# Plain-head attention scores as split products, with the rotary parts stacked on both halves of the partitions

## What is computed

```python
def mla_attention(q_nope, q_pe, k_nope, k_pe, v):
    scale = (q_nope.shape[-1] + q_pe.shape[-1]) ** -0.5

    def block(args):
        qn, qr = args
        s = (jnp.einsum('bqhd,bkhd->bhqk', qn, k_nope)
             + jnp.einsum('bqhr,bkr->bhqk', qr, k_pe)).astype(jnp.float32) * scale
        p = jax.nn.softmax(s, axis=-1).astype(v.dtype)
        return jnp.einsum('bhqk,bkhd->bqhd', p, v)
```

## Time and profile before

| | us |
|---|---|
| median of 3 runs | 2017.85 |
| lowest and highest | 2015.47, 2018.05 |
| profiled execution, its own time | 2011.72 |
| its span in the profile | 2009.9 |
| mean granted clock | 0.995 |
| busy: PE, DVE, ACT, POOL | 1893.5, 762.4, 612.0, 628.7 |

### The profile page before, as it was taken

How to read it: one execution, slowest core, us unless ns; L and a number is a source line. 1 busy time by engine, 2 the same in 40 slices (tenths; PEclk the granted TensorE clock), 3 DMA queues, 4 the chain that set the end, 5 groups by cost and what they waited for, 6 DMA issues and landing times.

```text
span 2009.9 us, 22143 instructions
## 1 busy us (share of the span) xinstructions
PE 1893.5 (94%) x8716; PEld 1220.1 (61%) x8716; DVE 762.4 (38%) x1551; ACT 612.0 (30%) x1111; POOL 628.7 (31%) x374
## 2 busy tenths in 40 slices
PE   5999999999989989989999999899899999999998
PEld 3554337634333333368887868544577678888786
DVE  6552266523222222262899225366340220000002
ACT  3112562311011011062223344466343342232212
POOL 0000432011011010054443325555434235555532
PEclk9999999999999999999999999999999999999999
DMA  9452003889999999963224321110142023322321
GB/s 383 168 211 87 32 22 131 316 359 426 428 427 427 428 428 428 396 217 111 84 84 126 105 84 67 49 33 22 64 157 84 1 95 101 109 84 88 122 84 63
DMA packets 90037, 358.29 MB, mean 178 GB/s; under 512 B 6955, under 2 KB 35883, under 8 KB 75484
## 3 DMA queue, kind: packets, MB, share of 16 engines
q1 hardware_dynamic: 87088, 351.75, 45.1%
q0 software_dynamic: 2304, 4.20, 0.6%
q10 hardware_dynamic: 556, 1.13, 0.1%
HBM read 355.42 MB, written 5.83 MB: 180 GB/s over the span
## 4 chain that ended last, share of the span: by engine, by line
PE 75%; DMA 13%; DVE 5%; ACT 3%; issue 2%; POOL 1%; SPq 0%; POOLq 0%; DVEq 0%; ACTq 0%
PE bank L754 14%; PE bank L756 14%; PE bank L755 14%; PE bank L729 11%; DMA slots<-in_w_expert_gate 9%; PE bank L1160 7%; DMA slots<-in_w_expert_up 3%; PE bank L1373 2%; PE bank L1393 2%; PE bank L881 1%; PE bank L1362 1%; PE bank L1131 1%; PE bank L1185 1%; ACT area L1983 1%; DMA slots<-in_w_ada 1%
## 5 line engine op out<-in xcount | busy, mean ns | idle before, releaser
L2815 POOL TENSOR_TENSOR low_r<-slots,high_r 128x2048 fp32r<-128x2048 f32 x82 | 380.0, 4634 | 511.1 <-ACT high_r L1612 511.1
L755 PE MATMUL bank<-xl_r,high_r 128*128 128x512 f32 (+1 forms) x832 | 320.3, 385 | 0.0
L754 PE MATMUL bank<-area_r,high_r 128*128 128x512 f32 x800 | 312.7, 391 | 0.0
L756 PE MATMUL bank<-area_r,low_r 128*128 128x512 f32 x800 | 311.3, 389 | 0.0
L1612 ACT ACTIVATE high_r<-slots 128x2048 fp32r<-128x2048 f32 x82 | 156.9, 1914 | 402.9 <-PE bank L756 402.1
L1160 PE MATMUL bank<-slots,area 128*64 128x512 f32 x992 | 226.8, 601 | 22.5 <-DMA slots<-in_w_expert_gate 16.2
L755 PEld LDWEIGHTS bank<-xl_r,high_r 128*128 128x128 f32 x832 | 156.3, 188 | 31.6 <-issue 0.5
L756 PEld LDWEIGHTS bank<-area_r,low_r 128*128 128x128 f32 x800 | 150.2, 188 | 31.5
L754 PEld LDWEIGHTS bank<-area_r,high_r 128*128 128x128 f32 x800 | 150.2, 188 | 31.4 <-issue 0.6
L1160 PEld LDWEIGHTS bank<-slots,area 128*64 128x64 f32 x992 | 67.5, 137 | 165.4 <-issue 126.0
L2616 DVE SCALAR_TENSOR_TENSOR bank<-area,cols,bank 128x512 f32<-128x512 f32 x232 | 153.4, 747 | 0.0
(11 more groups left out here) (423 smaller groups left out, 2811.7 us busy)
## 6 DMA issues: line engine op xcount, KB each, us to landing
slots<-in_w_expert_down SPq DMA_DIRECT2D x32, 2048.0 KB, 16.3
slots<-in_w_expert_up SPq DMA_DIRECT2D x32, 2048.0 KB, 16.2
slots<-in_w_expert_gate SPq DMA_DIRECT2D x30, 2048.0 KB, 15.0
slots<-in_w_in SPq DMA_DIRECT2D x15, 2048.0 KB, 7.9
slots<-in_w_ada SPq DMA_DIRECT2D x11, 2048.0 KB, 12.0
slots<-in_ffn_in_w SPq DMA_DIRECT2D x22, 1024.0 KB, 6.7
slots<-in_ffn_out_w SPq DMA_DIRECT2D x5, 2048.0 KB, 7.8
slots<-in_w_out SPq DMA_DIRECT2D x4, 2048.0 KB, 8.1
```

What stands on the lines that cost most here:

```text
L754: nc.tensor.matmul(out, xh, yh, start=start and n == 0, stop=False)
L755: nc.tensor.matmul(out, xh, yl, start=False, stop=False)
L756: last = nc.tensor.matmul(out, xl, yh, start=False, stop=stop and n == len(pairs) - 1)
L2815: nc.gpsimd.tensor_tensor(low_half(m), raw_half(m), high_half(m), ALU.subtract).then_inc(s["w_low"], 1)
```

## The change

The plain and rotary scores become five products of the rounded type. A plain query and key are each kept as a high and a low part, and give three products. The rotary query of a head stands on both halves of the partitions, the upper 64 partitions (0 to 63) as high part and the other 64 as low part, and the rotary key stands on both halves as a high part in one tile and as a low part in another; two products 128 deep then give all four combinations.

For this, `rope_twice` writes each rotated query twice, side by side, and four rotary tiles, one for each head, are transposed instead of two. ScalarE makes the high parts (the eight plain tiles, the rotary key, the four rotary tiles) and no longer frees their banks; VectorE subtracts each from the bank to get the low part, and frees the bank. The wait ahead of the first score is for VectorE's emptying of the eight query and key groups and of all four rotary tiles. Nine semaphores of one-off requests between VectorE and ScalarE are replaced by two shared ones with higher counts, and two transfers' semaphores are merged with others (their waits take the summed count). The rest of the loop, the differential heads, and all later stages are as they were.

```diff
-plan("up", ["dve"] * 4 + ["act"] * 12, 1, 2)
+plan("up", ["dve"] * 12 + ["act"] * 4, 1, 2)
...
-for _stage, _n in (("norm1", KT), ("latents", 4), ("kpe", 1), ("dq", 4), ("dk", 4), ("qpe", 2), ("mem0", KT // 2), ("norm2", KT),
+for _stage, _n in (("norm1", KT), ("latents", 4), ("kpe", 1), ("dq", 4), ("dk", 4), ("qpe", 4), ("mem0", KT // 2), ("norm2", KT),
...
+ASKED = {"lam": 2, "latents": 3, "router_group": 4, "router_expert": 5, "layer_norm": 6}
+GIVEN = {"csil": 1, "latents": 2, "lam": 3, "router_group": 4, "router_expert": 5, "layer_norm": 6}
...
-                    ("area0_r", 4096), ("area1_r", 8432 - 4096), ("area2_r", FT * C)))
+                    ("area0_r", 4096), ("area1_r", 8432 - 4096), ("area2_r", 22016 - 8432)))
...
-        QN = A(16896, 2048, 4)
+        QNS = (AR(16896, 2048, 4), AR(5120, 2048, 4))
         RQ = A(18944, 2048, TT)
-        KN = A(18944, 2048, 4)
+        KNS = (AR(18944, 2048, 4), AR(2048, 2048, 4))
         RT = A(20992, C)
-        QPE = A(20992, 1024, 2)
+        QPS = xl_r[:, 2048:4096].rearrange("p (h n) -> p h n", h=4)
+        KPS = (AR(20992, C), AR(21504, C))
         BADA = E(4096, 2048, 4)
         ada_acc = E(2048, 2048, 4)
         XN1 = E(4096, 4096, TT)
-        QRT = E(0, 1024, TT)
+        QRT = E(0, 2048, TT)
...
-            transpose_tokens("qpe", QRT, 2)
+            transpose_tokens("qpe", QRT, 4)
...
                 if t < 16:
-                    n, a = t, 64 * (h % 2)
+                    n, tokens = t, slice(i * P, (i + 1) * P)
                     if n >= 4:
                         pe.wait_ge(s["exp_done"], n - 3)
                     accumulate(banks[SCORE_BANK[n % 4]][:, :],
-                               [(QN[:, h, i * P:(i + 1) * P], KN[:, h, :]),
-                                (QPE[a:a + 64, h // 2, i * P:(i + 1) * P], KPE[a:a + 64, :])]
+                               [(QNS[0][:, h, tokens], KNS[0][:, h, :]), (QNS[0][:, h, tokens], KNS[1][:, h, :]),
+                                (QNS[1][:, h, tokens], KNS[0][:, h, :]),
+                                (QPS[:, h, tokens], KPS[0]), (QPS[:, h, tokens], KPS[1])]
                                ).then_inc(s["scores_full"], 1)
...
-            pe.wait_ge(s["act_emptied"], emptied("act", FIRST["up"] + 11))
-            pe.wait_ge(xpose_emptied[0], (XP["qpe"] + 3) // 2)
-            pe.wait_ge(xpose_emptied[1], (XP["qpe"] + 2) // 2)
+            pe.wait_ge(s["dve_emptied"], emptied("dve", FIRST["up"] + 11))
+            transposed_emptied(XP["qpe"] + 4)
...
-            act.wait_ge(s["latent_var"], 1)
-            nc.scalar.activation(stdc, varc, ACT.Sqrt).then_inc(s["latent_std"], 1)
+            act.wait_ge(s["asked_of_act"], ASKED["latents"])
+            nc.scalar.activation(stdc, varc, ACT.Sqrt).then_inc(s["given_by_act"], 1)
...
             g = FIRST["up"]
             for h in range(4):
-                empty(nc.scalar.activation(QN[:, h, :], full(g + 4 + h)[:, :], ACT.Copy, scale=MLA_SCALE))
+                nc.scalar.activation(QNS[0][:, h, :], full(g + 4 + h)[:, :], ACT.Copy, scale=MLA_SCALE
+                                     ).then_inc(s["up_high"], 1)
             for h in range(4):
-                empty(nc.scalar.activation(KN[:, h, :], full(g + 8 + h)[:, :], ACT.Copy))
-            for c in range(2):
-                n = XP["qpe"] + c
-                nc.scalar.activation(QPE[:, c, :], transposed(n)[:, :], ACT.Copy, scale=MLA_SCALE
-                                     ).then_inc(xpose_emptied[n % 2], 1)
+                nc.scalar.activation(KNS[0][:, h, :], full(g + 8 + h)[:, :], ACT.Copy).then_inc(s["up_high"], 1)
+            act.wait_ge(s["rope_ready"], 4 * TT)
+            nc.scalar.activation(KPS[0], KPE, ACT.Copy).then_inc(s["up_high"], 1)
+            for h in range(4):
+                nc.scalar.activation(QPS[:, h, :], transposed(XP["qpe"] + h)[:, :], ACT.Copy, scale=MLA_SCALE
+                                     ).then_inc(s["up_high"], 1)
             act.wait_ge(s["mod_biased"], 4)
...
+            def rope_twice(g, t, out):
+
+                bank = full(g)
+                cosines, sines = RT[:, 256:512], RT[:, 0:256]
+                dve.wait_ge(s["rope_ready"], ropes[0])
+                ropes[0] += 1
+                nc.vector.tensor_tensor(cosines.rearrange("p (h b) -> p h b", b=32),
+                                        bank[:, 0:256].rearrange("p (h b) -> p h b", b=32),
+                                        bass.AP(late, K2_COS + t * 32, [[1024, P], [0, 8], [1, 32]]), ALU.mult)
+                nc.vector.tensor_tensor(sines.rearrange("p (h a b) -> p h a b", a=2, b=32),
+                                        bass.AP(bank, 32, [[C, P], [64, 4], [-32, 2], [1, 32]]),
+                                        bass.AP(late, K2_SIN + t * 64, [[1024, P], [0, 4], [32, 2], [1, 32]]), ALU.mult
+                                        ).then_inc(s["dve_emptied"], 1)
+                dve.wait_ge(s["dve_emptied"], emptied("dve", g))
+                nc.vector.tensor_tensor(out.rearrange("p (h a b) -> p h a b", h=4, a=2),
+                                        bass.AP(area, 20992 + 256, [[22016, P], [64, 4], [0, 2], [1, 64]]),
+                                        bass.AP(area, 20992, [[22016, P], [64, 4], [0, 2], [1, 64]]), ALU.add
+                                        ).then_inc(s["rope_ready"], 1)
...
-            dve.wait_ge(s["lam_exp"], 1)
+            dve.wait_ge(s["given_by_act"], GIVEN["lam"])
             then(nc.vector.tensor_tensor(lamv[:, 4:5], lamv[:, 3:4], lamv[:, 2:3], ALU.subtract))
             then(nc.vector.tensor_scalar(lamv[:, 5:6], lamv[:, 4:5], -LAMBDA_INIT, None, ALU.add))
             for t in range(TT):
-                rope(FIRST["up"] + t, t, 4, QRT[:, t, :])
+                rope_twice(FIRST["up"] + t, t, QRT[:, t, :])
+            for h in range(8):
+                out, factor = (QNS, MLA_SCALE) if h < 4 else (KNS, 1.0)
+                dve.wait_ge(s["up_high"], h + 1)
+                nc.vector.scalar_tensor_tensor(out[1][:, h % 4, :], full(FIRST["up"] + 4 + h)[:, :], factor,
+                                               out[0][:, h % 4, :], ALU.mult, ALU.subtract).then_inc(s["dve_emptied"], 1)
+            dve.wait_ge(s["up_high"], 9)
+            nc.vector.tensor_tensor(KPS[1], KPE, KPS[0], ALU.subtract)
+            for h in range(4):
+                n = XP["qpe"] + h
+                dve.wait_ge(s["up_high"], 10 + h)
+                nc.vector.scalar_tensor_tensor(QPS[64:128, h, :], banks[6 + n % 2][64:128, :], MLA_SCALE, QPS[64:128, h, :],
+                                               ALU.mult, ALU.subtract).then_inc(xpose_emptied[n % 2], 1)
...
-                        dve.wait_ge(s["fg2_loaded"], 16)
+                        dve.wait_ge(s["router_loaded"], 64)
...
```

More of the change, by code:

```diff
@@ L436, in build @@
         names = ["w_loaded0", "w_loaded1", "w_loaded2", "w_loaded3", "cols_loaded", "x_loaded", "consts",
-                 "proj_done", "act_emptied", "dve_emptied", "ones_set", "ada_acc", "norm1_ready",
-                 "act_step", "dve_step", "csil_ready",
+                 "proj_done", "act_emptied", "dve_emptied", "ones_set", "ada_acc", "norm1_ready", "up_high",
+                 "act_step", "dve_step", "asked_of_act", "given_by_act",
                  "ssq_ready", "var_ready", "std_ready", "xn_ready", "xpose_full", "bank6_emptied", "bank7_emptied",
-                 "latent_var", "latent_std", "latents_ready", "rope_ready",
-                 "lam_ready", "lam_exp", "scores_full", "exp_done", "max_ready", "rcp_ready", "scaled",
+                 "latents_ready", "rope_ready",
+                 "scores_full", "exp_done", "max_ready", "rcp_ready", "scaled",
                  "probs_mla", "probs_diff", "pt_full", "pt_ready", "pv_full", "pv_emptied",
@@ L1334, in _ @@
             split_emptied("mix")
-            pe.wait_ge(s["cmp_bias_loaded"], 64)
+            pe.wait_ge(s["extras_loaded"], 128)
             for h in range(NH):
@@ L1667, in _ @@
                                      ).then_inc(xpose_emptied[n % 2], 1)
-            act.wait_ge(s["lam_ready"], 2)
-            nc.scalar.activation(lamv[:, 2:4], lamv[:, 0:2], ACT.Exp).then_inc(s["lam_exp"], 1)
+            act.wait_ge(s["asked_of_act"], ASKED["lam"])
+            nc.scalar.activation(lamv[:, 2:4], lamv[:, 0:2], ACT.Exp).then_inc(s["given_by_act"], 1)
             act.wait_ge(s["bias_stored"], 16)
@@ L1777, in _ @@
                                      ).then_inc(xpose_emptied[n % 2], 1)
-            act.wait_ge(s["router_exp_in"], 1)
-            nc.scalar.activation(RS(144, 16), RS(144, 16), ACT.Exp).then_inc(s["router_exp_out"], 1)
-            act.wait_ge(s["router_exp_in"], 2)
-            nc.scalar.activation(RS(1284, 4), RS(1280, 4), ACT.Exp).then_inc(s["router_exp_out"], 1)
+            act.wait_ge(s["asked_of_act"], ASKED["router_group"])
+            nc.scalar.activation(RS(144, 16), RS(144, 16), ACT.Exp).then_inc(s["given_by_act"], 1)
```

(18 more changed lines are left out.)

18 lines of the change are left out of this document (9 added, 9 removed).

## The result

| | before | after |
|---|---|---|
| median, us | 2016.66 (4 runs) | 2003.57 (4 runs) |
| lowest and highest | 2014.86, 2018.05 | 2000.96, 2006.36 |
| profiled execution | 2011.72 | 2006.36 |
| span | 2009.9 | 2004.5 |

The ratio is 0.9939, with a 95% interval of 0.992 to 0.9958: 8.5 to 16 us faster, 13.1 by the medians.

A forecast was written before the change was run, and what follows sets the result against it. TensorE's plain matmuls were taken to bound the plain heads, their gain passing to the end one for one: -13.2 + 3.2 + 0.3 + 0.8 = -8.9 us, from 2017.85 to 2009.0 us, range 2004.9 to 2013.8.

The forecast's parts named there:

- pause ahead of the value groups: Before the value groups, TensorE waits for banks VectorE returns late, starting them near 194.0 instead of 190.77: 3.2 us lost.
- doubled rotation and low parts, ahead of the rotary tiles: Ahead of the rotary transposes, VectorE's extra work is covered by the eight query and key groups (13.8 us): costs nothing.
- sixteen score units, with their transposes: Plain heads' loop: first four units save 3.7 us, the other twelve 9.5; together 13.2 us if TensorE stays the bound.
- wait for GpSimd in the loop: In step 9 of the loop, a head's low part (1.27 us) comes before the scaling; TensorE waits 0.3 us.
- the way through the differential heads: Behind the plain heads, the latency-bound part starts from the same state as now: no change.
- the clock: After the stretch 190.93 to 194.0 the granted clock may fall, costing 1.7 us; half, 0.8, taken.
- switch: At the first rounded product after fp32 transposes, 0.08 us more to the next start; five products 1.14, with it 1.22.
- the present fall at 294.7: Clock fall at the output product at 294.19 (5.29 us instead of 3.60); may come or not, another 1.7 to gain.
- A: Plain heads' loop: the other engines, ScalarE (1.78) and GpSimd (1.96), bound it; -4.1 us, 2013.8; chance 0.16.
- B: Plain heads' loop keeps 2.5 us a step through a hidden ring of kept tile, exponential, scaling, transpose; +4.9, 2022.8; chance 0.05.
- C: Plain scores' products run at an fp32 product's 0.86 us instead of as the rounded type; 2058; chance 0.01.

The follow-up runs named there:

- the two repeated runs: The kernel before and the changed kernel, each measured and profiled once more without an edit; ratios 0.9996 and 0.9941 to the kernel before.
- spread kernel: Changed kernel with the third and fourth rotary tiles transposed between the second and third value group; ratio 0.9938 to the kernel before.
- halves: Changed kernel with its two rotary products cut to the first 64 rows; ratio 0.9971 to the kernel before.
- plain only: Changed kernel with the rotary part undone: one fp32 product 64 rows deep, two rotary tiles, old rotation; ratio 0.9984 to the kernel before.
- rotary only: Changed kernel with the plain part undone: one fp32 product a unit, stacked rotary pair kept; ratio 0.9956 to the kernel before.
- the bound at two: Changed kernel with only one plain and one rotary high-part product, three of five products left out; ratio 0.9918 to the kernel before.
- before, again: The kernel before, measured and profiled once more without an edit; ratio 0.9996 to the kernel before.

## Why the prediction was right in kind and short in size

Term by term, with the two repeated runs, which have no fall of the clock in the stretch (18.06 to the value groups, 70.71 to the first differential score before; 21.17 and 59.78 after):

| term | forecast | measured |
|---|---|---|
| pause ahead of the value groups | +3.2 | +3.1 (21.17 - 18.06) |
| doubled rotation and low parts, ahead of the rotary tiles | 0 | 0.01 (17.19 - 17.18, within the line above) |
| sixteen score units, with their transposes | -13.2 | -14.4 (38.61 - 52.65 - 0.38) |
| wait for GpSimd in the loop | +0.3 | +0.38 |
| the way through the differential heads | 0 | 0.00 (63.06 both times) |
| the clock | +0.8 | 1.7 or nothing, by the execution |
| sum up to the projection | -8.9 | -10.93 |

- **What bounds the kernel.** Right. The plain heads' loop was TensorE's (all but some six microseconds of it in the changed kernel, by the chain), and the differential heads took 63.06 us before and after: the time saved in the loop didn't come back as waits.
- **The pause.** Right in cause, place and size, as the chain of the changed kernel and the spread kernel show.
- **The score unit.** This is the step of the sum that failed, by its size. "Five are 1.14 us, with the switch 1.22", put behind transposes taken as fixed at 0.49, made a step of 1.71; it is 1.60. In recorded starts the transposes are 0.35 and the five products 1.25 (1.13 in a run without transposes). Two things make the 0.14 by which the transposes shrank. One is 0.06 that is really gone: with a rounded product behind them they take 0.41 where a product 64 rows deep stands before them (halves, plain only) and 0.35 where it is 128 deep, so the old unit's change of depth cost its neighbour too. The other is 0.08 that is only moved: a rounded product behind fp32 transposes is recorded that much sooner than an fp32 one (0.41 against 0.49, 0.35 against 0.43 in rotary only), and the next start pays it back. The "switch" of 0.08 was this payment, so the sum counted it without what stands against it. With 0.03 the other way (1.25 for 1.22) that is the 0.11 a step. Twelve such steps make 1.3 us, and the term is off by 1.2.
- **The clock.** The 0.8 for a fall behind the pause was a fair price on average (two falls in five profiles, 1.7 each: 0.7), but in one execution it is 1.7 or nothing. And I reckoned with two places, that one and the present fall at 294.7, as if the others stood still. They don't: the kernel before loses 8.6 us in one execution and 10.3 in another, the changed one 13.7 and 8.6. The first profile of after happened to have eight falls, the first of before five; with 10.9 us from the structure and 5.2 back for three more falls, that is about why the two executions are only 5.4 us apart and the medians 13.1.
- **The range, and the rest of the miss.** The median lies 5.4 us below the forecast. The sum accounts for 2.0 of it (8.9 for 10.93: 1.2 by the score units, and the 0.8 put in for the clock), the starting point for 1.2 (three runs with a median of 2017.85, four with 2016.66), and 2.2 are left. The lower end of the range took one fall and the spread of the three runs below their median. In the two later measurements the kernel before has medians of 2014.30 (17 runs) and 2015.26 (22 runs); 10.93 us below these is 2003.4 and 2004.3, both under the range, and the changed kernel's runs lie 5.4 us apart in the first measurement. A range of 4 us downwards was too narrow for an effect known to 1 us and a measurement that scatters by 3.
- **The rivals.** A: TensorE waited once, 0.38 us; not the bound at five products, the bound at two. What TensorE then waits for is GpSimd's scaling in SBUF, not the emptying of PSUM that the Trainium skill's rule names (TensorEngine Tiling (Array Packing), PSUM Bottleneck). In the loop no trace here shows that rule at work; a bank that comes back late holds TensorE only in the pause, for 1.84 us, because its emptying now takes two engines. B and C: steps of 1.60 and rounded products some 0.23 apart exclude them.
- **Still open.** The measured ratios of the changed kernel, 0.9939 and 0.9941, mean 12.3 and 11.9 us; the structure gives 10.9 up to the projection and nothing behind it (9.8 at the output in the one pair). The intervals (the second one 9.1 to 14.5 us) hold 10.9 and 9.8. Whether the remaining one to two microseconds are chance, or a schedule that draws fewer falls of the clock, these profiles can't tell.

## What to carry to other kernels

Where a short contraction is stacked so that all products have the full depth, count the removed change of depth in the unit itself (0.43 us here) and in what follows it (0.06 here), and take a "switch" between two kinds of product from a distance across both neighbours. Where new parts are subtracted from a transposition bank, ask when the bank comes back, and put independent products into that gap by order; here that took the whole pause away in the trace, 2.2 us, which the medians were too coarse to show. And before a change of half a per cent is forecast, look at how much the clock costs in two profiles of the same kernel: that scatter belongs in the range.

## What the hardware showed beyond expectation

- Each fall of the granted clock to 0.50 takes about 1.72 us (1.68 to 1.72 by the windows), in all ten profiles, four to eight of them in an execution of this kernel up to TensorE's last product. They come at certain places of the program, not in every execution: near 40 us in all ten; between 372 and 392 in nine of ten, once or twice; behind the pause in two of five. The one at the output product at 294.7 in the first profile is missing in before, again, and is back in rotary only at the same product (at 285.26 there). TensorE waits 1.52 or 1.53 us for VectorE ahead of that product in all ten, and two of them have the fall.
- Depth alone, 64 rows instead of 128 in two of five products, made a unit 0.43 us longer, 0.21 of it at the two and 0.21 at the three products of full depth.
- A rounded product behind fp32 ones is recorded as starting 0.40 us sooner (value groups to first score 6.47 instead of 6.87 in the changed kernel), and the next start is as much later, so distances have to be taken across both. Behind fp32 transposes the shift is 0.08.
